# One hybrid decoder layer: index keys and queries projected first, scores inside the third chunk, top-k rounds spread over the projection chunks

## The chip, the cores and the metric

The kernel runs on one core of one Trainium2 chip. The metric is the device time of one execution in microseconds (us), median of the runs of a kernel. Five engines work side by side, each through its own instructions in order: TensorE (PE in the profile, its weight loads PEld), VectorE (DVE), ScalarE (ACT), GpSimd (POOL) and SyncE (SP), which here only issues DMAs. They wait for each other through semaphores alone.

## The reference, cut to what matters

One layer over x (1, 512, 1024): h = RMSNorm(x), one projection h @ w_in of 7,000-odd columns, three token mixers side by side, gates, two output products. Mixer A picks keys with a small indexer; its part is

```python
A_HEADS, A_HEAD_DIM, IDX_HEADS, IDX_DIM, TOPK_MAX = 4, 64, 8, 64, 256
a_q, a_ckv, a_qi, a_ki, a_wi, a_z = split_cols(a_part, A_COLS)
topk = min(TOPK_MAX, s // 4)                                  # 128 of 512
idx_logits = jnp.einsum('bqhd,bsd->bqhs', qib, k_idx) * (IDX_DIM ** -0.5)
score = jnp.einsum('bqh,bqhs->bqs', wb * (IDX_HEADS ** -0.5), jax.nn.relu(idx_logits))
score = jnp.where(key_pos[None, None, :] <= t[None, :, None], score, NEG_INF)
_, sel = lax.top_k(score, topk)
kg, vg = k[bidx, sel], v[bidx, sel]                           # then softmax over the picked keys
```

Mixer B is a gated DeltaNet (a short causal convolution over 12 x 128 features, then a chunked delta rule over 4 chunks of 128 tokens), mixer C an attention over compressed, selected and windowed keys. Everything of A's selection is used only in A's attention, near the end.

## The kernel before

The order of the work is written out by hand, engine by engine, in one function `trunk`. Nothing is scheduled by a program, so each engine does exactly what stands in its block, in that order.

**Projections.** The columns of w_in are cut into chunks of 260 to 512 columns (`CHUNKS`). A chunk has four pieces of weights. For each piece SP loads it into one of three `stage` buffers (`load`), ScalarE scales it and rounds it to float16 (`hi_split`, L688 and L693), GpSimd subtracts to get the rest (`lo_split`, L459), and TensorE multiplies with both parts (`project`, `product`, L1443 to L1445: three matmuls for each of 8 slices, four tiles t = 0 to 3 for a chunk). After tile t of a chunk ScalarE drains its bank (`drain`) and then splits pieces of the next chunk (`FOLLOW`: one, one, two, none). The order of the chunks before is C0, C1, A0, QI, A2, B0, B1, B3, B4, B2, then six gate chunks (L1656 to L1660) that serve as filler (`fill`) in the DeltaNet and attention stages. QI holds the index queries, A2 the index keys (`kiT`) and index weights.

**Banks.** PSUM has eight banks. TensorE uses them in rings of two: `S` (banks 0 and 1, drained by ScalarE), `G` (2 and 3), `V` (4 and 5, drained by VectorE) and `O` (6 and 7). Every use of a ring has a number. `v_bank(name)` makes TensorE wait until VectorE has drained the use two places before, and `filled(name)` makes VectorE wait until that use is written. So TensorE can be at most two uses of `V` ahead of VectorE.

**Uses of V in the projections.** In order: transposes of the C queries and keys (`cqT0`, `cqT1`, `kcmp`, `vcmp`, `ksT`, `kwT`), `ckvT`, `qT0`, `qT1`, four key-and-value products `ukv` (L1547, copied out by L1009 and L1010), `kT0`, `kT1` (scaled out by L1026), `kiT` (L1027), eight `flip` products that reverse the bias strips (L1562, copied out by L1029), the compressed keys and values `cmpkv` (L1577, L1065), `kcT`, and `sums`, the bank of the square sums and cumulative decays (L1619, L1633, L1634). `phi` (L1517) is a small product between tiles that uses banks 2 and 3.

**Index scores.** After B0, TensorE makes 24 products of index queries and keys (L1572: 8 heads for each of three query blocks q = 1, 2, 3 with 256, 384 and 512 keys) in ring S; ScalarE takes the ReLU into one of two buffers (L681), VectorE multiplies with the weight and adds (L1039, L1041). GpSimd masks the diagonal (L510).

**Top-k.** `topk(q)` takes 16 rounds for each q: the eight largest of a row (`max`, L1084), then their places marked (`match_replace`, L1087, which also issues a MATCH_VALUE_LOAD); each waits for the one before it. Two closing operations (L1091, L1092) make the mask `keep_add`. Before, q = 1 stands between the convolutions of B0 and B1, q = 2 and q = 3 stand in the DeltaNet: 16 and 6 half rounds ahead of its start (`TOPK_A`, `TOPK_B`), the rest one by one between the steps of a level (`between_steps`).

**Convolutions.** `conv(m)` is one L1055 and three L1057 on VectorE, then a SiLU on ScalarE (L756); conv(0) to conv(3) need B0, 4 to 7 need B1, 8 to 11 need B2. `conv(m)` waits for the SiLU of m - 2.

**Start of the DeltaNet.** After the square sums, VectorE works through a chain of small operations (L1129 to L1146), `difference(0)` (L1160), conv(8) to conv(11), `decayed_products(0)` and `level_zero(0)` (L1179), which TensorE waits for before the first level (L1588).

Of the kernel before, what the change touches and what calls it, by code (L numbers as in the profile page):

```python
# [8 lines left out]
P = 128  # L9
T, D = 512, 1024  # L10
NT, KC = T // P, D // P
EPS = 1e-6
NEG = -1e30
# [22 lines left out]
    ("w_in", C_BASE, 448), ("w_in", C_VSEL, 460),  # L36
    ("w_in", A_Q, 384), ("w_in", A_QI, 512), ("w_in", A_KI, 328),
# [10 lines left out]
(CH_C0, CH_C1, CH_A0, CH_QI, CH_A2, CH_PK, CH_PV, CH_B0, CH_B1, CH_B3, CH_B4, CH_B2,  # L48
# [7 lines left out]

FILL_Z, FILL_U, FILL_X, FILL_T = 7, 2, 7, 3

TOPK_A, TOPK_B = 16, 6
# [9 lines left out]
def shape_constants():  # L69
# [13 lines left out]
    m = np.zeros((P, 2 * LEVELS, P), np.float16)  # L83
# [39 lines left out]
def trunk(nc, x, norm_g, w_in, a_kv_norm, a_w_ukv, a_q_norm, a_k_norm, b_conv, b_a_log, b_dt_bias, b_out_norm,  # L123
# [3 lines left out]
    u8 = mybir.dt.uint8  # L127
    ALU = mybir.AluOpType
# [3 lines left out]
    with ctx:  # L132
# [58 lines left out]
        mask_halves = late[:, 3456:3456 + LEVELS * P].bitcast(f16).rearrange("p (n m) -> p n m", m=P)  # L191
# [13 lines left out]
        scores = [late[:, 0:256], late[:, 3072:3456], early[:, 4608:5120]]  # L205
        topk_work = [early[:, 5120:5632], early[:, 5632:6144]]
# [22 lines left out]
        s_names = [(c, t) for c in ("C0", "C1", "A0", "QI", "A2", "B0") for t in range(4)]  # L229
        s_names += [("idx", q, h) for q in range(1, NT) for h in range(IDX_HEADS)]  # L230
        s_names += [(c, t) for c in ("B1", "B3", "B4", "B2") for t in range(4)]
# [8 lines left out]
        v_names += ["cqT0", "cqT1", "kcmp", "vcmp", "ksT", "kwT"]  # L240
        v_names += ["ckvT", "qT0", "qT1"] + [("ukv", t) for t in range(NT)] + ["kT0", "kT1", "kiT"]
# [20 lines left out]
        O = Uses(banks[6:8], [("os", c) for c in range(1, NT)] + [("oc", n) for n in range(2)] + [("o", *g) for g in groups])  # L262
# [27 lines left out]
        T_IN = Steps(sem("transpose_input_ready"), ["C0q", "C0blk", "C0ks", "C1kw", "A0ckv", "A0q", "Ak", "Aki", "kc"])  # L290
# [60 lines left out]
        order = [(c, j) for c in range(CH_A2 + 1) for j in range(4)]  # L351
        for v, c in ((CH_PK, CH_B0), (CH_PV, CH_B1)):
            order += [(v, 0), (c, 0), (v, 1), (c, 1), (v, 2), (c, 2), (c, 3), (v, 3)]
        order += [(c, j) for c in range(CH_B3, len(CHUNKS)) for j in range(4)]
# [43 lines left out]
        def _(sp):  # L398
# [18 lines left out]
            for n in range(piece_at[CH_WO0, 0]):  # L417
                if n == piece_at[CH_C1, 3]:
# [3 lines left out]
                h = n - piece_at[CH_QI, 0]  # L422
# [5 lines left out]
                if n == piece_at[CH_A0, 2]:  # L428
                    sp.dma_start(mask_halves, masks).then_inc(masks_loaded, 16)
# [15 lines left out]
        def _(gp):  # L445
# [23 lines left out]
            for j in range(4):  # L469
                lo_split(CH_C0, j)  # L470
# [3 lines left out]
            for t in range(4):  # L474
                follow(CH_C0, t)
# [17 lines left out]
            for t in range(4):  # L493
                follow(CH_QI, t)
# [4 lines left out]
            for c in (CH_A2, CH_B0):  # L499
                for t in range(4):  # L500
                    follow(c, t)
                if c == CH_A2:

                    gp.wait_ge(masks_loaded, 16)
                    hold(gp.tensor_copy(level_masks[:, :, :], mask_halves))

            for q in range(1, NT):
                gp.wait_ge(score_ready, q)
                d = scores[q - 1][:, P * q:P * q + P]
                gp.affine_select(out=d, in_=d, compare_op=ALU.is_ge, fill=NEG, base=0, pattern=[[-1, P]],  # L510
                                 channel_multiplier=1).then_inc(diag_ready, 1)
# [11 lines left out]
            def masked_decays(c):  # L523

                gp.wait_ge(exp_ready, c + 1)
                hold(gp.tensor_tensor(decay_k, decay, over_heads(tri), ALU.mult))
# [115 lines left out]
        def _(act):  # L642
# [71 lines left out]
            def h_hi(t):  # L714
                for a in range(2):
                    if t < 2:
                        hi_split(CH_C0, 2 * t + a)
# [6 lines left out]
            for t in range(4):  # L724
                drain(("C0", t), raw_c0[:, t, :], 448, scale=1.0 / W_SCALE)
                follow(CH_C0, t)
                if t == 0:
                    h_hi(3)
# [5 lines left out]
            drain_chunk(CH_QI, "QI", lambda t: qiT[:, t, :], 384)  # L734
            drain_chunk(CH_A2, "A2", lambda t: raw_a2[:, t, :], 328)
            sqrt("Ak", ss_k, 16)
            act.wait_ge(fills, 3)
            drain_chunk(CH_B0, "B0", lambda t: qkvT[:, t, 3:T + 3])
            act.wait_ge(hid_filled, 1)
            for h in range(2):  # L740
                ins = nc.scalar.activation(hidT[:, h::2, :], banks[2 + h][:, 0:2 * N_CMP].rearrange("p (v n) -> p v n", v=2), ACT.Silu)
            ins.then_inc(hid_ready, 1)

            n = 0
            for q in range(1, NT):
# [132 lines left out]
        def _(ve):  # L878
# [141 lines left out]
            for a in range(2):  # L1020
                ins = ve.tensor_copy(ki2[:, :, a, :], raw_a2[:, :, 0:64])
# [834 lines left out]
```

## Time and profile before

| | us |
|---|---|
| median of 3 runs | 718.66 |
| lowest, highest | 716.79, 718.68 |
| the profiled execution | 722.38 |
| its span, first to last instruction | 720.5 |
| TensorE busy in it | 655.4 |
| VectorE busy in it | 451.1 |
| ScalarE, GpSimd busy in it | 310.6, 233.1 |

The profile is of one execution. Its span is 1.9 us shorter than that execution's device time, and the execution is 3.7 us above the median. Busy time is the sum over an engine's instructions; matmuls are pipelined, so the end of one is modelled and overlaps the start of the next by about 0.16 us in the timelines. What a wait is put down to is inferred from semaphores; "DVEq" is VectorE's own sequencer, which passes a semaphore on.

### The profile page before, as it was taken

How to read it: one execution, taken by the hardware profiler on the slowest of the kernel's cores; microseconds unless marked ns; L12 is line 12 of the kernel's file. 1: busy time of each engine (PE TensorE's matmuls, PEld its weight loads, DVE VectorE, ACT ScalarE, POOL GpSimd, SP SyncE). 2: the span in 40 equal slices, each digit the busy share in tenths (PEclk: the TensorE clock that was granted, in tenths of full speed). 3: DMA queues.
4: the chain of work that ended last, by engine and by line, in shares of the span. 5: the costliest groups of instructions: out<-in, count | busy, mean ns of one | idle time of the engine just before them, and what ended most of it. 6: DMA issues, size and time to landing. Idle time of an engine off the chain costs nothing.

```text
span 720.5 us, 9726 instructions
## 1 busy us (share of the span) xinstructions
PE 655.4 (91%) x3650; PEld 396.6 (55%) x3650; DVE 451.1 (63%) x897; ACT 310.6 (43%) x502; POOL 233.1 (32%) x165
## 2 busy tenths in 40 slices
PE   2799899999999984989999999999999999788898
PEld 1345556654358642767676787655555556433343
DVE  6623442314799989887878655335777775689711
ACT  3554442424556844604415122544555545253510
POOL 1353533312044644313434301434321121132530
PEclk9999899999999997999999989899999999999999
DMA  7235414532024202010200201100110120242221
GB/s 272 79 118 169 144 50 144 160 106 71 2 60 131 89 30 88 4 56 0 89 30 10 80 1 30 59 30 30 60 31 30 58 60 1 58 176 87 88 88 59
DMA packets 31191, 52.78 MB, mean 73 GB/s; under 512 B 2759, under 2 KB 13345, under 8 KB 31145
## 3 DMA queue, kind: packets, MB, share of 16 engines
q1 hardware_dynamic: 29552, 51.19, 22.6%
q10 hardware_dynamic: 1593, 0.97, 0.5%
q8 instruction: 29, 0.48, 0.3%
q14 instruction: 17, 0.14, 0.1%
HBM read 50.04 MB, written 2.12 MB: 72 GB/s over the span
## 4 chain that ended last, share of the span: by engine, by line
PE 63%; DVE 26%; issue 4%; ACT 3%; DMA 2%; POOL 1%; SPq 0%; DVEq 0%; ACTq 0%
PE bank L1588 7%; PE bank L1443 7%; PE bank L1444 7%; PE bank L1445 7%; PE bank L1656 5%; PE bank L1658 5%; PE bank L1660 5%; PE bank L1746 5%; PE bank L1763 4%; DVE early L1057 4%; DVE early L1087 3%; DVE small L1084 3%; DVE work L1179 3%; PE bank L1517 2%; PE bank L1782 2%
## 5 line engine op out<-in xcount | busy, mean ns | idle before, releaser
L459 POOL TENSOR_TENSOR w_lo<-stage,w_hi 128x1024 f16<-128x1024 f32 (+5 forms) x80 | 159.2, 1996 | 259.2 <-ACT w_hi L693 258.9
L1588 PE MATMUL bank<-work 128*128 128x128 f32 x616 | 81.3, 282 | 11.7 <-DVEq L1154 11.4
L1588 PEld LDWEIGHTS bank<-work 128*128 128x128 f32 x616 | 77.1, 195 | 23.7 <-DVEq L1154 17.9
L693 ACT ACTIVATE w_hi<-stage 128x1024 f16<-128x1024 f32 (+5 forms) x80 | 78.3, 979 | 19.9 <-issue 14.9
L688 ACT ACTIVATE stage<-stage 128x1024 f32<-128x1024 f32 (+5 forms) x80 | 77.4, 968 | 3.3 <-DMA stage<-in_w_in 3.3
L1656 PE MATMUL bank<-hT_hi,w_hi 128*128 128x512 f16 x192 | 74.6, 388 | 1.7 <-PE bank L1660 0.6
L1658 PE MATMUL bank<-hT_lo,w_hi 128*128 128x512 f16 x192 | 74.5, 388 | 0.5
L1660 PE MATMUL bank<-hT_hi,w_lo 128*128 128x512 f16 x192 | 74.3, 387 | 0.3
L1443 PE MATMUL bank<-w_hi,hT_hi 128*128 128x260 f16 (+4 forms) x192 | 62.0, 323 | 6.0 <-DVE hT_lo L923 3.0
L1444 PE MATMUL bank<-w_lo,hT_hi 128*128 128x260 f16 (+4 forms) x192 | 61.6, 321 | 0.0
L1445 PE MATMUL bank<-w_hi,hT_lo 128*128 128x260 f16 (+4 forms) x192 | 61.6, 321 | 0.0
L841 ACT ACTIVATE late<-late,small 128x128 f32<-128x128 f32 (+3 forms) x48 | 26.8, 558 | 53.7 <-DVE small L1325 53.7
L1443 PE MATMUL bank<-hT_hi,w_hi 128*128 128x512 f16 (+1 forms) x128 | 49.0, 383 | 0.8 <-ACT qkvT L681 0.4
L1444 PE MATMUL bank<-hT_lo,w_hi 128*128 128x512 f16 (+1 forms) x128 | 49.1, 383 | 0.0
L1445 PE MATMUL bank<-hT_hi,w_lo 128*128 128x512 f16 (+1 forms) x128 | 48.8, 382 | 0.0
L1179 DVE COPY_PREDICATED work<-level_masks,bank 128x512 f32<-128x512 uint8 x48 | 35.1, 732 | 21.4 <-PE bank L1588 14.6
L1361 DVE RECIPROCAL qkvT<-qkvT 128x128 f32<-128x128 f32 x48 | 45.7, 953 | 1.6
L681 ACT ACTIVATE late<-bank 128x256 f32<-128x256 f32 (+3 forms) x72 | 31.1, 449 | 17.4 <-PE bank L1572 9.7
L1057 DVE SCALAR_TENSOR_TENSOR early<-qkvT,par,early 128x512 f32<-128x512 f32 x36 | 36.7, 1019 | 1.3
L710 ACT ACTIVATE early<-bank 128x512 f32<-128x512 f32 x12 | 7.2, 597 | 67.8 <-PE bank L1660 67.8
L1443 PE MATMUL bank<-strips,w_hi 128*128 128x512 f16 x64 | 25.1, 392 | 9.7 <-DVE qkvT L1388 4.2
L1322 DVE CUSTOM_DVE_ANT_0 late<-bank,strips 128x128 f32<-128x128 f32 (+3 forms) x36 | 16.9, 469 | 25.7 <-PE bank L1746 23.6
(281 smaller groups left out, 1183.6 us busy)
## 6 DMA issues: line engine op xcount, KB each, us to landing
stage<-in_w_in SPq DMA_DIRECT2D x40, 512.0 KB, 3.5
stage<-in_c_phi_w SPq DMA_DIRECT2D x8, 512.0 KB, 3.9
stage<-in_w_branch SPq DMA_DIRECT2D x8, 512.0 KB, 3.7
stage<-in_w_out SPq DMA_DIRECT2D x8, 512.0 KB, 3.7
stage<-in_w_in SPq DMA_DIRECT2D x8, 260.0 KB, 2.8
strips<-rel_rows SPq DMA_DIRECT2D x8, 256.0 KB, 4.0
late<-in_x SPq DMA_DIRECT2D x1, 2048.0 KB, 8.9
out_x<-late SPq DMA_DIRECT2D x8, 256.0 KB, 2.2
```

The costliest lines, as they stand in the source:

```text
L459: gp.tensor_tensor(piece_view(w_lo[:, k % PAIRS, :], c), piece_view(stage[:, piece_at[c, j] % STAGES, :], c), piece_view(w_hi[:, k % PAIRS ...
L688: nc.scalar.activation(full, full, ACT.Copy, scale=W_SCALE).then_inc(scaled, 1)
L693: nc.scalar.activation(piece_view(w_hi[:, k % PAIRS, :], c), full, ACT.Copy).then_inc(hi_ready, 1)
L1057: ins = ve.scalar_tensor_tensor(acc, qkvT[:, m, w:w + T], tap[w], acc, ALU.mult, ALU.add)
L1179: return ve.copy_predicated(dst, level_masks[:, n, :].unsqueeze(1).to_broadcast([P, 4, P]), src)
L1443: mm(ps, lhs[0], rhs[0], start=start, stop=False)
L1444: mm(ps, lhs[0], rhs[1], start=False, stop=False)
L1445: return mm(ps, lhs[1], rhs[0], start=False, stop=stop)
L1588: ins = mm(ps[:, h * P:(h + 1) * P], lhs(h), rhs(h), start=True, stop=True)
L1656: mm(G.bank(g)[:, :], w[0], h[0], start=k == 0, stop=False)
L1658: mm(G.bank(g)[:, :], w[0], h[1], start=False, stop=False)
L1660: ins = mm(G.bank(g)[:, :], w[1], h[0], start=False, stop=k == KC - 1)
```

## The change

- The chunks A2 (index keys and weights) and QI (index queries) are projected first. The order is A2, QI, C0, C1, A0, B0, B1, B3, B4, B2. The orders of loads, of ScalarE's and of GpSimd's splits follow. The weights of `phi` are loaded among the pieces of B1 and B3 (before, of B0 and B1), and its products stand between the tiles of B0 and B1 (before, of A2 and B0).
- The 24 index products stand inside C0: after each of the first four slices of its tiles 0, 1 and 2, two of them, in ring O instead of S. Before C0, TensorE waits for the transposed index keys.
- The C transposes stand after tiles 2 and 3 of A0, `ckvT` after tile 2 of B0, `qT0`, `qT1` and all four `ukv` after tile 3 of B0, `kT0` and `kT1` after tile 1 of B1, the flips after its tiles 2 and 3, four each. `cmpkv` follows B3, `kcT` follows B4.
- A round of top-k is one step (max and match together), a q has 17 steps. They stand on VectorE as 17 after the scores (all of q = 1), 8 after the A0 queries are normalised, 6 between the `qT` and `ukv` copies, 6 after the `ukv` copies, 6 after the `kT` copies, and the last 8 after the flips. None is left in the DeltaNet. The buffers of scores and rounds move from `early` to `late`; `masked_decays(0)` on GpSimd waits for the last round.
- conv(0) and conv(1) stand ahead of the `kT` copies, conv(2) and conv(3) among the flip copies, conv(4) and conv(5) ahead of `cmpkv`, conv(6) and conv(7) behind its chain. The square root `kc` on ScalarE stands after tile 1 of B4.
- The level masks are loaded as uint8 straight into place, at B0; before, as float16 with a cast on GpSimd (L505).

```diff
-    ("w_in", C_BASE, 448), ("w_in", C_VSEL, 460),
-    ("w_in", A_Q, 384), ("w_in", A_QI, 512), ("w_in", A_KI, 328),
+    ("w_in", A_KI, 328), ("w_in", A_QI, 512),
+    ("w_in", C_BASE, 448), ("w_in", C_VSEL, 460), ("w_in", A_Q, 384),
...
+TOPK_C, TOPK_A0, TOPK_UKV, TOPK_AK, TOPK_KT = 17, 8, 6, 6, 6
...
-TOPK_A, TOPK_B = 16, 6
...
+            def index_relu(n):
+                q, h = idx_units[n]
+                if n >= 2:
+                    act.wait_ge(relu_used, n - 1)
+                L = P * (q + 1)
+                act.wait_ge(o_filled, O.filled(("idx", q, h)))
+                nc.scalar.activation(relu_buf[n % 2][:, 0:L], O.bank(("idx", q, h))[:, 0:L], ACT.Relu).then_inc(o_drained, 1)
+
             for t in range(4):
+                for n in range(8 * t, min(8 * t + 8, len(idx_units))):
+                    index_relu(n)
                 drain(("C0", t), raw_c0[:, t, :], 448, scale=1.0 / W_SCALE)
...
+            drain_chunk(CH_B1, "B1", lambda t: qkvT[:, 4 + t, 3:T + 3], between=lambda t: silus(t, {1: (0, 1), 2: (2,), 3: (3,)}))
...
+            def between_b4(t):
+                silus(t, {0: (4, 5), 2: (6, 7)})
+                if t == 1:
+                    sqrt("kc", ss_kc[0:N_CMP, :], 1)
...
+            def topk_all():
+
+                for q in range(1, NT):
+                    ve.wait_ge(diag_ready, q)
+                    src = scores[q - 1]
+                    for r in range(TOPK // 8):
+                        m8 = max8[:, 8 * (r % 2):8 * (r % 2) + 8]
+                        hold(ve.max(m8, src))
+                        dst = topk_work[r % 2][:, 0:P * (q + 1)]
+                        hold(ve.match_replace(dst, m8, src, TAKEN))
+                        src = dst
+                        yield
...
+            topk(TOPK_A0)
             ve.tensor_scalar(ckvT, filled("ckvT")[:, :], par[:, R_CKV:R_CKV + 1], None, ALU.mult).then_inc(v_drained, 1)
...
+            topk(TOPK_UKV)
...
+            topk(TOPK_AK)
             SQ.wait(ve, "Ak")
...
+            conv(0)
+            conv(1)
...
+            topk(TOPK_KT)
+            conv(2)
             for h in range(N_HEADS):
                 ve.tensor_copy(strips[:, h, :], filled(("flip", h))[:, :]).then_inc(v_drained, 1)
+                if h == N_HEADS // 2 - 1:
+                    conv(3)
...
+            for _ in topk_steps:
+                pass
+            conv(4)
+            conv(5)
...
+            def index_products(t, k):
+                if t == 3 or k > 3:
+                    return
+                for q, h in idx_units[8 * t + 2 * k:8 * t + 2 * k + 2]:
...
+            project(CH_C0, "C0", True, within=index_products)
```

VectorE around the copies of `ukv`. Before, the two `qT` copies, then the copies of the four products (L1009 and L1010 for each), in banks 4 and 5:

```order
L1001 TENSOR_SCALAR work<-bank5,par 128x512
L1003 TENSOR_SCALAR qT_a<-bank4,par 128x512
L1003 TENSOR_SCALAR qT_a<-bank5,par 128x512
L1009 COPY work<-bank4 128x256
L1010 COPY v_a<-bank4 128x256
L1009 COPY work<-bank5 128x256
```

In the change, the same place (L1070 is `qT`, L1077 and L1078 are the copies; the left-out rows are four more rounds like the two shown):

```order
L1070 TENSOR_SCALAR qT_a<-bank5,par 128x512
L1070 TENSOR_SCALAR qT_a<-bank4,par 128x512
L971 MAX small<-late 128x8
L973 MATCH_REPLACE late<-small,late 128x384
...
L971 MAX small<-late 128x8
L973 MATCH_REPLACE late<-small,late 128x384
L1077 COPY work<-bank5 128x256
L1078 COPY v_a<-bank5 128x256
```

Six rounds now stand between a drain of banks 4 and 5 and the next. TensorE at that place in the change (L1479 the `qT` transposes, L1566 `ukv`):

```order
L1479 MATMUL bank5<-consts,work 128x128 x4
L1479 MATMUL bank4<-consts,work 128x128 x4
L1566 MATMUL bank5<-work 128x512
L1566 MATMUL bank4<-work 128x512
L1566 MATMUL bank5<-work 128x512
L1566 MATMUL bank4<-work 128x512
L1443 MATMUL bank0<-hT_hi,w_hi 128x512
```

Its four products stand in a row, as before, but the tile of projection between the two transposes is gone, and B1's first tile stands behind them.

VectorE from the `kT` copies to the flip copies, before (L1026 `kT`, L1027 `kiT`, L1029 flips):

```order
L1026 TENSOR_SCALAR kT_a<-bank4,par 128x512
L1026 TENSOR_SCALAR kT_a<-bank5,par 128x512
L1027 COPY work<-bank4 128x512
L1029 COPY strips<-bank5 128x512
L1029 COPY strips<-bank4 128x512
```

and in the change (L957 and L959 are a convolution, L1089 `kT`, L1093 flips; the left-out rows are four more rounds):

```order
L957 TENSOR_SCALAR early<-qkvT,par 128x512
L959 SCALAR_TENSOR_TENSOR early<-qkvT,par,early 128x512 x3
L1089 TENSOR_SCALAR kT_a<-bank5,par 128x512
L1089 TENSOR_SCALAR kT_a<-bank4,par 128x512
L971 MAX small<-late 128x8
L973 MATCH_REPLACE late<-small,late 128x512
...
L971 MAX small<-late 128x8
L973 MATCH_REPLACE late<-small,late 128x512
L957 TENSOR_SCALAR early<-qkvT,par 128x512
L959 SCALAR_TENSOR_TENSOR early<-qkvT,par,early 128x512 x3
L1093 COPY strips<-bank5 128x512
```

Two convolutions came ahead of the `kT` copies, and six rounds and a convolution between them and the first flip copy.

## Rows read from the trace of the kernel before

**Rows 1.** TensorE's waits: waiting line, releaser, us in total, times, longest.
```profile
PE bank L1588 <- DVEq L1154: 11.4, 5, 7.6
```

**Rows 2.** Stretches: length, engines' busy time (instructions), granted clock, DMA share, GB/s.
```profile
98.50:172.50 74.00, 72.23 (x417) 44.52 (x415) 18.91 (x32) 27.64 (x37) 24.77 (x13) 0.98 0.43 126
...
172.50:191.00 18.50, 15.28 (x54) 7.00 (x54) 13.43 (x23) 10.01 (x24) 0.58 (x2) 1.00 0.04 14
...
284.00:288.00 4.00, 4.00 (x15) 2.44 (x15) 3.75 (x6) 1.02 (x2) 0.30 (x1) 0.55 0.38 127
```

**Rows 3.** TensorE's timeline: start, us, instruction, count, idle before and releaser.
```profile
283.57 2.08 PE L1588 MATMUL bank<-work 128*128 128x128 f32 x8 [7.59 <-DVEq L1154]
285.44 0.63 PE L1656 MATMUL bank<-hT_hi,w_hi 128*128 128x512 f16 x1
...
319.74 1.13 PE L1588 MATMUL bank<-work 128*128 128x128 f32 x8
...
321.14 0.38 PE L1656 MATMUL bank<-hT_hi,w_hi 128*128 128x512 f16 x1
```

**Rows 4.** Line L1084 and L1087 on VectorE: ns min/median/max, first to last start.
```profile
L1084 DVE MAX8 small<-early x46: 428/561/697, 209.2 to 396.6; 128x8 f32<-128x512 f32 x16, 128x8 f32<-128x256 f32 x15, 128x8 f32<-128x384 f32 x15
...
L1087 DVE MATCH_REPLACE8 early<-small,early x46: 408/543/678, 209.7 to 397.4; 128x512 f32<-128x512 f32 x16, 128x256 f32<-128x256 f32 x15, 128x384 f32<-128x384 f32 x15
```

**Rows 5.** VectorE's timeline: a round at 384 columns, and the next's start.
```profile
244.53 0.56 DVE L1084 MAX8 small<-late 128x8 f32<-128x384 f32 x1
...
245.78 0.56 DVE L1084 MAX8 small<-early 128x8 f32<-128x384 f32 x1
```

**Rows 6.** Timelines around the `ukv` products: TensorE, then VectorE.
```profile
107.94 4.11 PE L1547 MATMUL bank<-work 128*128 128x512 f32 x8
...
108.14 0.75 DVE L1003 TENSOR_SCALAR qT_a<-bank,par 128x512 f32<-128x512 f32 x1 [3.71 <-PE bank L1479]
109.07 0.42 DVE L1009 COPY work<-bank 128x256 f32<-128x256 f32 x1 [0.18 <-PE bank L1547]
...
114.84 1.22 DVE L1012 TENSOR_REDUCE small<-early 128x16 f32<-128x1024 f32 x1 [2.00 <-POOL early L498]
```

**Rows 7.** Timelines, B0's tile 1 to the flips: TensorE, then VectorE.
```profile
143.90 0.38 PE L1443 MATMUL bank<-hT_hi,w_hi 128*128 128x512 f16 x1
...
149.08 1.87 PE L1517 MATMUL bank<-early,stage 128*128 128x31 f32 x16
150.78 3.02 PE L1562 MATMUL bank<-strips,work 128*128 128x512 f32 x6
...
151.92 0.69 DVE L1029 COPY strips<-bank 128x512 f32<-128x512 f32 x1 [7.13 <-PE bank L1562]
```

**Rows 8.** Timelines at convolutions: VectorE, then a weight split on GpSimd.
```profile
228.70 4.07 DVE L1057 SCALAR_TENSOR_TENSOR early<-qkvT,par,early 128x512 f32<-128x512 f32 x3
232.69 0.48 DVE L1055 TENSOR_SCALAR early<-qkvT,par 128x512 f32<-128x512 f32 x1
233.21 2.33 DVE L1057 SCALAR_TENSOR_TENSOR early<-qkvT,par,early 128x512 f32<-128x512 f32 x3
...
229.15 2.29 POOL L459 TENSOR_TENSOR w_lo<-stage,w_hi 128x1024 f16<-128x1024 f32 x1 [4.27 <-ACT w_hi L693]
```

**Rows 9.** Timelines from `sums` to level zero: TensorE, then VectorE.
```profile
255.24 0.40 PE L1633 MATMUL bank<-small,consts 128*128 128x16 f32 x2 [1.03 <-DVEq L1125]
255.49 0.37 PE L1634 MATMUL bank<-small,ones 128*128 128x16 f32 x2
...
259.03 0.23 DVE L1129 COPY small<-bank 128x64 f32<-128x64 f32 x1
...
281.40 2.03 DVE L1179 COPY_PREDICATED work<-level_masks,work 128x512 f32<-128x512 uint8 x1
```

**Rows 10.** Page, part 6: DMA issues of weight pieces, KB each, us to landing.
```profile
stage<-in_w_in SPq DMA_DIRECT2D x40, 512.0 KB, 3.5
```

More of the change, by code:

```diff
@@ L127, in trunk @@
     u8 = mybir.dt.uint8
+    idx_units = [(q, h) for q in range(1, NT) for h in range(IDX_HEADS)]
     ALU = mybir.AluOpType
@@ L493, in _ @@
             for t in range(4):
-                follow(CH_QI, t)
+                follow(CH_B0, t)
             gp.wait_ge(v_drained, V.filled(("ukv", 3)))
@@ new lines, in _, with topk @@
+            topk_steps = topk_all()
+            def topk(n):
+                for _ in range(n):
+                    next(topk_steps)
+            ve.wait_ge(s_drained, S.filled(("A2", 3)))
+            ki2 = squares[:, 1024:1536].rearrange("p (t a d) -> p t a d", t=NT, a=2)
+            for a in range(2):
+                ins = ve.tensor_copy(ki2[:, :, a, :], raw_a2[:, :, 0:64])
+            ins.then_inc(T_IN.sem, 1)
+            hold(ve.tensor_scalar(raw_a2[:, :, 64:72], raw_a2[:, :, 64:72], IDX_HEADS ** -0.5, 64 ** -0.5, ALU.mult, ALU.mult))
@@ new lines, in _ @@
+            ve.tensor_copy(kiT, filled("kiT")[:, :]).then_inc(v_drained, 1)
+            ve.wait_ge(v_drained, V.filled("kiT"))
+            n = 0
+            for q in range(1, NT):
+                L = P * (q + 1)
+                for h in range(IDX_HEADS):
+                    ve.wait_ge(o_drained, O.filled(("idx", q, h)))
+                    r, wi = relu_buf[n % 2][:, 0:L], raw_a2[:, q, 64 + h:65 + h]
+                    if h == 0:
+                        ins = ve.tensor_scalar(scores[q - 1], r, wi, None, ALU.mult)
+                    else:
+                        ins = ve.scalar_tensor_tensor(scores[q - 1], r, wi, scores[q - 1], ALU.mult, ALU.add)
+                    n += 1
+                    ins.then_inc(relu_used, 1)
+                    ve.wait_ge(relu_used, n)
+                ve.nop().then_inc(score_ready, 1)
@@ L1117, in _ @@
             ve.nop().then_inc(GATE_IN.sem, 1)
-            for _ in range(TOPK_A):
-                next(topk_last)
+            ve.tensor_scalar(kcT[:, 0:N_CMP], filled("kcT")[:, 0:N_CMP], par[:, R_CK:R_CK + 1], None, ALU.mult).then_inc(v_drained, 1)
             GATE_OUT.wait(ve, "sp")
@@ L1125, in _ @@
             ve.nop().then_inc(gsum_ready, 1)
-            for _ in range(TOPK_B):
-                next(topk_last)
             ps = filled("sums")
@@ L1643, in _ @@
             project(CH_B4, "B4", True, between=between_b4)
+            T_IN.wait(pe, "kc")
+            transposes("kcT", [raw_c0[0:N_CMP, 0, 0:128]], N_CMP)
             project(CH_B2, "B2", False, between=between_b2, within=within_b2)
```

257 lines of the change are left out of this document (100 added, 157 removed).

## Prediction

> **What bounds the kernel now.** I read the shares of busy time first: TensorE is busy 655.4 of a span of 720.5 us, VectorE 451.1. So an edit counts only by what it does to TensorE's idle time. Then its waits: only five, 11.4 us in all, lie in the DeltaNet on VectorE's vector work, and one of them is 7.6 [rows 1]. Then the stretches that the change touches. Over 98.5 to 172.5 TensorE works 72.23 of 74.0 us and VectorE only 18.91; in the index scores TensorE works 15.28 of 18.50 [rows 2]. The tempting reading is that VectorE has 55 us to give away ahead of the scores. The other question is when VectorE must answer: TensorE may be only two uses of ring V ahead, and VectorE takes its instructions in order, so rounds put before a drain are paid for by whatever TensorE cannot cover with other work.
>
> **What a wait costs beyond itself.** After the 7.59 us wait TensorE's next two groups took 2.08 and 0.63 us, where elsewhere they took 1.13 and 0.38 [rows 3], and over the next 4 us the granted clock was 0.55 [rows 2], its lower level (1.2 GHz) for most of it. That is 4 x 0.45 = 1.8 us and 0.2 for the half us ahead of it: 2.0 us behind a long wait. I charge it to each wait of over 5 us.
>
> **What a round costs.** A max and a match have medians of 561 and 543 ns [rows 4]; a round of 384 columns has a pitch of 1.25 us [rows 5], so waits and the value load add 0.13. At 256 columns (0.43 + 0.41, row minima) it is 0.98, at 512 (0.70 + 0.68, maxima) 1.53. The last of a q also has two closing operations, about 0.8 (an estimate, two passes like those of a round at 384 columns, less their wait).
>
> **Wait A, `ukv`.** The two `qT` copies (0.75) are followed at once by the first `ukv` copy (0.42) in the trace; the four products take 4.11, 1.03 each [rows 6]. In the change six rounds (6 x 1.25 = 7.5) stand between. TensorE can write two products and must then wait for the copies of the first. From the second `qT` copy: VectorE 7.5 + 0.8 = 8.3, TensorE 1.0. +7.3, with the clock **+9.3**. Nothing covers it: the projection tile between the two transposes is gone, too.
>
> **Wait B, the flips.** From the last `ukv` product on, VectorE has its copies 0.8; two rounds 2.5, closing 0.8, three rounds 4.6; the key norms, with two passes of 1.22 [rows 6] and a root, about 4; conv(0) and conv(1); two `kT` copies 1.5; six rounds 9.2; conv(2); one flip copy 0.7 [rows 7]. A convolution is 0.48 + 2.28 = 2.76, from the 2.33 of three steps; beside a GpSimd split (2.29) the three took 4.07, so 1.74 more [rows 8]. With one such split that is 34.2 us. TensorE ahead of its third flip has three tiles of 5.2 (143.90 to 149.08 is one), three `phi` of 1.7, `kT` 0.9 and two flips of 0.95 [rows 7]: 23.5. +10.7, with the clock **+12.7**. Before, VectorE stood idle 7.13 us ahead of that copy, so this is a lead turned into a lag.
>
> **Wait C, `sums`.** Its bank is free only when `cmpkv` is copied. After the flips VectorE has seven more rounds 10.7, closing 0.9, conv(4) and conv(5) 5.5 with one split 1.75, and the copies: about 20. TensorE has B3, four tiles of 260 columns (5.2 x 260 / 512 = 2.64 each), `cmpkv` and flip rests 0.9, and B4's first tile 2.64: 14.1. +5.9, with the clock **+7.9**.
>
> **D, the root `kc`.** ScalarE takes it only after B4's tile 1, so VectorE, which has just caught up, stands still before conv(6) and conv(7); ScalarE's SiLU of those stands before its drain of B4's tile 3. From TensorE's release in C: root at about 7.5 (tile 1, drain, split: estimated), rest of the chain 1, two convolutions with one split 7.3, SiLUs and drain 2.0: 17.8. TensorE: sums 1.0, three tiles 7.9, `kcT` 0.3, B2's tile 0 5.2: 14.4. +3.4, and 0.9 for a last piece of B2 whose ScalarE half is late: **+4.3**, from 0 to 6.
>
> **Index scores.** The 3.2 us of waits [rows 2] go and another 0.3 of overlap with C0's slices; new are ScalarE's weight splits ahead of a ReLU at tiles 1 and 2, and VectorE's accumulations beside GpSimd's splits. By rows 8 the nearest such meeting cost 1.74; bounds 0.5 and 3, I take 1.7. **-1.8**. What the trace shows here is the 4.07 against 2.33 [rows 8]: steps with two inputs in SBUF slow down beside GpSimd, and the one-input L1055 at 232.69 ran 0.48. The Trainium skill, page "SBUF — State Buffer", section "Who interferes with whom", states just that: two SBUF inputs contend with a GpSimd instruction that reads SBUF, one input does not. It speaks against moving the scores beside C1's and C0's splits; without it this term would be about -3.0, with it -1.8.
>
> **Start.** The first chunk has 120 columns less, one tile of it 1.2 us shorter (5.2 x 120 / 512) before the second can wait for weights: -1.2. QI's last piece (load 3.5 [rows 10], GpSimd split 2.29) queues behind GpSimd's other splits: +1.5. TensorE waits for the `kiT` copy before C0: 0.7 and its semaphores, +1.0. **+1.3**, from -1 to +3, since no row shows this order.
>
> **What goes.** The small waits of 98.5 to 172.5 are 74.0 - 72.2, **-1.8** [rows 2], as their drains lie elsewhere. The VectorE chain that ends in level zero (283.43) began on `sums` at 259.03 though TensorE had it ready at 255.86, and TensorE had waited 1.03 for the bank [rows 9]: half rounds stood in between and are gone, **-4.2**. The rest of that chain stays, so TensorE still waits some us for level zero. The other four DeltaNet waits are 11.4 - 7.6 = 3.8 [rows 1]; no round is left in those stages: **-3.5**. The other rounds removed there are worth nothing, as TensorE works through them. Masks as uint8, the loads' order and the steps of a round: nothing, all behind TensorE's work (a mask load that came late would hold level zero; it has over 100 us).
>
> **Sum.** 9.3 + 12.7 + 7.9 + 4.3 = 34.2; -1.8 + 1.3 - 1.8 - 4.2 - 3.5 = -10.0; +24.2. Against the profiled 722.4 that is 746.6. That execution is 3.7 above the median of 718.7; on the median's basis **742.9**.
>
> **The rivals.** *Shorter waits*: the three waits come, but the clock does not drop behind them and D finds cover: 24.2 - 6.0 - 4.3 = 13.9, 732.6. For: 7.6 us is the only wait whose clock I can read. Against: nothing differs in kind.
>
> *Longer*: up to six more GpSimd splits fall on convolutions and accumulations, 6 x 1.74 = 10.4: 753. For: GpSimd splits nearly without a pause in the projections. Against: half of VectorE's new work there is rounds, and rows 4 show none slowed by more than a fourth.
>
> *Faster, the other side*: VectorE drains each bank before TensorE comes. It rests on one balance, wait B's 34.2 against 23.5; it turns if rounds and convolutions there take under two thirds of my price, or TensorE's share is half as large again. Then A and C, smaller balances of the same kind, would vanish first, and only -10.0 is left: 708.7. For: VectorE's 18.91 of 74.0 [rows 2]. Against: the listed instructions, each with its row.
>
> *Cancelling*: A alone comes at full size (TensorE has nothing else there) and meets the gains: 9.3 - 10.0, 718.
>
> **How the numbers follow.** Forecast 742.9 with its own range 735 to 750, chance 0.60; shorter 728 to 735, 0.17; longer to 753, 0.11; faster 0.07; cancelling 0.05. The range takes the first three, 728 to 753. A measurement of this kernel tells about 0.3% (2.2 us) from no change: faster 0.07, same 0.03 (most of cancelling), slower 0.90.
>
> **What would show it.** In the changed kernel's trace: the third `ukv` product idle about 7 us before it, the third flip about 11, the first square sum after B4's tile 0 about 6, B2's tile 1 about 3; a low clock for some 4 us behind each of the first three; the DeltaNet's waits down from 11.4 to about 8; under 2 us of idle between the index products. I would be wrong in kind if TensorE shows no wait on VectorE at these places, and in size if convolutions measure far from 2.76 or rounds from 1.25.

## The result and the profile after

The changed kernel takes 741.25 us (median of 4 runs, 739.46 to 741.38) against 718.67 before: a ratio of 1.0294, 95% interval 1.0251 to 1.0336, slower by 22.6 us. The forecast was 742.9 with a range of 728 to 753. The profiled execution of the change is 739.46 us, its span 737.6, against 722.38 and 720.5 before: the two traces differ by 17.1, the medians by 22.6. Some executions of a kernel are slower by a per cent or two as a whole, at a lower granted clock (728.27 among those before); medians here are of all executions, ratios and intervals of the undisturbed ones alone.

The page has the same work and more idle time: TensorE 654.2 us busy (655.4 before), in a span 17.1 longer.

```profile
span 737.6 us, 9700 instructions
...
PE 654.2 (89%) x3650; PEld 398.5 (54%) x3650; DVE 449.8 (61%) x897; ACT 310.2 (42%) x502; POOL 236.9 (32%) x164
```

TensorE's waits of the change (waiting line, releaser, total, times, longest) answer to [rows 1]; the longest, 10.8 us for a DMA near the start, is left out, since the kernel before has it too (10.6). L1566 is `ukv`, L1580 the flips, L1628 the first square sums, L1443 with `raw_b` is B2's tile 1, L1597 the DeltaNet.

```profile
PE bank L1580 <- DVE strips L1093: 10.2, 1, 10.2
PE bank L1597 <- DVEq L1159: 8.8, 3, 7.6
PE bank L1566 <- DVE v_a L1078: 6.8, 1, 6.8
PE bank L1628 <- DVE cmp_v L1105: 6.0, 1, 6.0
...
PE bank L1443 <- ACT raw_b L678: 3.6, 1, 3.6
```

The four new waits are there with sizes near the computed ones (7.3, 10.7, 5.9 and 3.4). TensorE's timeline of the change shows each, and what the next group took:

```profile
164.19 1.96 PE L1566 MATMUL bank<-work 128*128 128x512 f32 x4 [0.50 <-DVE qT_a L1070]
172.92 3.43 PE L1566 MATMUL bank<-work 128*128 128x512 f32 x4 [6.78 <-DVE v_a L1078]
...
197.75 1.96 PE L1580 MATMUL bank<-strips,work 128*128 128x512 f32 x4
209.91 3.71 PE L1580 MATMUL bank<-strips,work 128*128 128x512 f32 x4 [10.20 <-DVE strips L1093]
...
244.98 6.99 PE L1628 MATMUL bank<-ones,early 128*128 128x1 f32 x32 [6.02 <-DVE cmp_v L1105]
...
273.69 0.39 PE L1443 MATMUL bank<-hT_hi,w_hi 128*128 128x512 f16 x1 [3.63 <-ACT raw_b L678]
...
308.80 2.08 PE L1597 MATMUL bank<-work 128*128 128x128 f32 x8 [7.59 <-DVEq L1159]
```

The same two products take 1.96 us ahead of a wait and 3.43 or 3.71 behind it. The last row answers to the first of [rows 3]: the first level begins at 308.80 instead of 283.57, 25.2 us later, with the same 7.59 us of waiting ahead of it.

### The profile page after: what moved, and what is told of

It reads as the page before. It is cut to its first block, busy times and chain, and to the rows that moved or that the text cites. A ratio compares the mean times of both kernels' runs of the same rounds, so it can differ in the third digit from the quotient of the medians.

```text
span 737.6 us, 9700 instructions
## 1 busy us (share of the span) xinstructions
PE 654.2 (89%) x3650; PEld 398.5 (54%) x3650; DVE 449.8 (61%) x897; ACT 310.2 (42%) x502; POOL 236.9 (32%) x164
## 4 chain that ended last, share of the span: by engine, by line
PE 70%; DVE 21%; issue 3%; ACT 2%; DMA 1%; POOL 1%; SPq 0%; DVEq 0%; ACTq 0%
PE bank L1597 11%; PE bank L1443 8%; PE bank L1445 7%; PE bank L1444 7%; PE bank L1667 6%; PE bank L1669 6%; PE bank L1671 5%; PE bank L1757 5%; PE bank L1774 4%; DVE early L959 4%; DVE late L973 2%; DVE small L971 2%; PE bank L1793 2%; PE bank L1479 2%; PE bank L1628 1%
## 5 line engine op out<-in xcount | busy, mean ns | idle before, releaser
L457 POOL TENSOR_TENSOR w_lo<-stage,w_hi 128x1024 f16<-128x1024 f32 (+5 forms) x80 | 162.3, 2036 | 297.6 <-ACT w_hi L690 297.6
L690 ACT ACTIVATE w_hi<-stage 128x1024 f16<-128x1024 f32 (+5 forms) x80 | 78.3, 979 | 32.7 <-issue 28.7
L1597 PE MATMUL bank<-work 128*128 128x128 f32 x616 | 79.4, 278 | 9.1 <-DVEq L1159 8.8
L1597 PEld LDWEIGHTS bank<-work 128*128 128x128 f32 x616 | 77.1, 193 | 17.7 <-DVEq L1159 10.7
L1443 PE MATMUL bank<-w_hi,hT_hi 128*128 128x260 f16 (+4 forms) x192 | 63.3, 330 | 3.6 <-DVE hT_lo L928 2.2
L1443 PE MATMUL bank<-hT_hi,w_hi 128*128 128x512 f16 (+1 forms) x128 | 47.3, 370 | 6.5 <-ACT raw_b L678 3.6
L1445 PE MATMUL bank<-hT_hi,w_lo 128*128 128x512 f16 (+1 forms) x128 | 47.3, 370 | 0.0
L1444 PE MATMUL bank<-hT_lo,w_hi 128*128 128x512 f16 (+1 forms) x128 | 47.3, 370 | 0.0
L959 DVE SCALAR_TENSOR_TENSOR early<-qkvT,par,early 128x512 f32<-128x512 f32 x36 | 39.9, 1108 | 1.3
L1443 PE MATMUL bank<-strips,w_hi 128*128 128x512 f16 x64 | 24.9, 389 | 9.3 <-DVE qkvT L1388 4.2
L1322 DVE CUSTOM_DVE_ANT_0 late<-bank,strips 128x128 f32<-128x128 f32 (+3 forms) x36 | 16.9, 469 | 26.7 <-PE bank L1757 24.6
L1443 PEld LDWEIGHTS bank<-w_hi,hT_hi 128*128 128x128 f16 x192 | 19.7, 103 | 22.5 <-issue 8.8
```

The costliest lines, as they stand in the source:

```text
L457: gp.tensor_tensor(piece_view(w_lo[:, k % PAIRS, :], c), piece_view(stage[:, piece_at[c, j] % STAGES, :], c), piece_view(w_hi[:, k % PAIRS ...
L690: nc.scalar.activation(piece_view(w_hi[:, k % PAIRS, :], c), full, ACT.Copy).then_inc(hi_ready, 1)
L959: ins = ve.scalar_tensor_tensor(acc, qkvT[:, m, w:w + T], tap[w], acc, ALU.mult, ALU.add)
L1443: mm(ps, lhs[0], rhs[0], start=start, stop=False)
L1444: mm(ps, lhs[0], rhs[1], start=False, stop=False)
L1445: return mm(ps, lhs[1], rhs[0], start=False, stop=stop)
```

## Why TensorE waits there

VectorE's timeline of the change, from the `qT` copies to the copies of `ukv`: the start of the first and the whole of the last of the six rounds, which fill 164.62 to 172.07, and then the first of the two copies for which TensorE waits.

```profile
163.29 1.41 DVE L1070 TENSOR_SCALAR qT_a<-bank,par 128x512 f32<-128x512 f32 x2 [6.92 <-PE bank L1479]
164.62 0.55 DVE L971 MAX8 small<-late 128x8 f32<-128x384 f32 x1
...
170.86 0.56 DVE L971 MAX8 small<-late 128x8 f32<-128x384 f32 x1
171.46 0.09 DVE L973 MATCH_VALUE_LOAD late<-small,late 128x8 f32 x1
171.53 0.54 DVE L973 MATCH_REPLACE8 late<-small,late 128x384 f32<-128x384 f32 x1
172.11 0.42 DVE L1077 COPY work<-bank 128x256 f32<-128x256 f32 x1
```

VectorE stood idle for 6.92 us just ahead of the `qT` copies, and then started six rounds when TensorE needed it. The pitch (from one round's start to the next's) is 1.25, as in [rows 5]. The second place is in front of B2, on VectorE and then on ScalarE:

```profile
245.44 0.14 DVE L897 TENSOR_SCALAR small<-small 31x1 f32<-31x1 f32 x1
261.19 0.15 DVE L904 RECIPROCAL small<-small 31x1 f32<-31x1 f32 x1 [15.60 <-ACT small L674]
```

```profile
257.22 0.39 ACT L678 ACTIVATE raw_b<-bank 128x260 f32<-128x260 f32 x1 [11.89 <-PE bank L1445]
...
260.96 0.20 ACT L674 ACTIVATE small<-small 31x1 f32<-31x1 f32 x1
```

VectorE asked for the root `kc` at 245.44 and had it at 261.19. ScalarE was idle for 11.89 us of that, since tile 1's drain stands ahead of the root in its order, and TensorE, released from its wait at 244.98, ended tile 1 only at 257.2: the square sums and the tile, both at a low clock, took 12.2 us.

## Experiments

The runs that change one thing start from the changed kernel (741.2). Each was run beside the kernel before, whose medians were 718.5, 721.5 and 718.3 in the three sets, so a difference of under 2 or 3 us between kernels of different sets tells nothing.

### The six rounds put behind the `ukv` copies

```diff
-TOPK_C, TOPK_A0, TOPK_UKV, TOPK_AK, TOPK_KT = 17, 8, 6, 6, 6
+TOPK_C, TOPK_A0, TOPK_UKV, TOPK_AK, TOPK_KT = 17, 8, 0, 12, 6
```

> The changed kernel with one move on VectorE: the six rounds between the qT and the ukv copies stand behind the ukv copies, with the six that are there already. Theory (VectorE is late as a whole from ukv to the flips, so rounds moved within that stretch only move the wait): the wait before the third ukv product falls from 6.8 us to under 0.5, and its low clock (1.5) goes, but the wait before the third flip grows from 10.2 by the six rounds, 7.5, to about 17.7; net -0.6 to -1.5, about 740 us against the changed kernel's 741.2. Rival (each drain behind rounds costs by itself, the flips have cover for more): 741.2 - 8.3 = 733.

Measured 741.62 us, ratio 1.0353 (1.0286 to 1.042). TensorE's timeline (the last row ends where its view ended; the fourth product is not in it):

```profile
168.04 4.00 PE L1566 MATMUL bank<-work 128*128 128x512 f32 x8 [0.50 <-DVE qT_a L1070]
192.09 1.97 PE L1479 MATMUL bank<-consts,work 128*128 128x128 f32 x8 [6.28 <-DVE work L1085]
213.09 2.92 PE L1580 MATMUL bank<-strips,work 128*128 128x512 f32 x3 [8.52 <-DVE strips L1093]
```

The wait at `ukv` is gone and stands elsewhere: 6.3 ahead of the `kT` transposes, whose norms VectorE computes late, and 8.5 at the flips, 14.8 in all against 17.0. The rival's 733 lies outside the interval. The theory held in sum; that a part would fall on `kT` was not foreseen.

### The six rounds put ahead of the `qT` copies

```diff
+            topk(TOPK_UKV)
             for m in range(2):
                 ve.tensor_scalar(qT_a[:, m, :], filled(f"qT{m}")[:, :], ...
...
-            topk(TOPK_UKV)
```

> The changed kernel with the same six rounds moved the other way, ahead of the qT copies, where VectorE stands idle 6.9 us (156.4 to 163.3). Theory (what costs is the place behind which VectorE cannot catch up): the 6.8 us wait and 1.5 us of low clock go, the rounds (7.5) overrun the idle stretch by 0.6; the other waits stay as they are: 741.2 - 8.3 + 0.6 = 733.5 us. Rival (VectorE has too much work in sum, the wait turns up at qT or at the flips): 740 to 741.

Measured 736.03 us, ratio 1.0274 (1.0198 to 1.035). The wait at `ukv` is gone, the wait ahead of the first product is 1.0 instead of the change's 0.5, and the waits at flips and sums are unchanged (10.2 and 6.0). The gain of 5.2 lies nearer the theory, but runs of 731.2 to 741.5 do not exclude the rival by time; the waits do.

### Half of them

Three rounds ahead of the `qT` copies, three left.

> The changed kernel with three of the six rounds ahead of the ukv copies put ahead of the qT copies: half of wait A. Theory: the wait before the third ukv product is what the rounds ahead of it take, less one product: 6.8 - 3.75 = 3.0 us, and the other three rounds lie in VectorE's idle 6.9 us, free. If a wait of 3 us costs no low clock behind it, the kernel gains 3.75 + 1.5 + 0.5 (the wait that was 0.5 ahead of it stays): 736; if it costs the same low clock, 3.75: 737.5. Rival (the wait has another cause than these rounds): 6 us or more stay, 741.

Measured 734.65 us, ratio 1.0221 (1.016 to 1.0281). The row of the wait in TensorE's timeline, and under it windows of 4 us (length, busy time of PE, PEld, DVE, ACT and POOL, granted clock, DMA share, GB/s):

```profile
168.68 3.49 PE L1567 MATMUL bank<-work 128*128 128x512 f32 x4 [3.02 <-DVE v_a L1079]
```

```profile
163.00:167.00 4.00, 2.08 (x6) 0.67 (x4) 3.86 (x9) 0.00 (x0) 0.00 (x0) 1.00 0.70 198
167.00:171.00 4.00, 2.32 (x3) 1.18 (x4) 2.42 (x8) 0.00 (x0) 0.00 (x0) 0.67 0.00 0
```

The wait is 3.0, as computed: round for round. The two products behind it still took 3.49, so this 3 us wait cost 1.5 of low clock too. The time alone would say the contrary (736 without that cost, 737.5 with it), but it also lies below that of the kernel with all six rounds moved, so differences of this size are not told apart by it; the row decides.

### The root `kc` earlier

```diff
-                if t == 1:
+                if t == 0:
                     sqrt("kc", ss_kc[0:N_CMP, :], 1)
```

> The changed kernel with one move on ScalarE: the square root kc stands after tile 0 of B4 instead of tile 1. Theory: VectorE no longer stands still for 15.6 us ahead of conv(6) and conv(7), so their SiLUs no longer hold ScalarE's drain of B4's tile 3; TensorE's waits at B2's tile 1 (3.6) and for the last weight piece of B2 (1.1) go, with the low clock behind them (about 2.5): -4.7 to -7.2, 734 to 736.5 us. Rival (the drain is late through ScalarE's own queue of splits, not through kc): within 1 us of 741.2.

Measured 733.49 us, ratio 1.0255 (1.0179 to 1.0331), 7.8 below the change and a little more than the 4.7 to 7.2 expected. Both waits in B2 are gone from the trace; wait C stands at 6.0 as before. The rival falls.

### The rounds spread over VectorE's idle stretches, and with the early root

```diff
-TOPK_C, TOPK_A0, TOPK_UKV, TOPK_AK, TOPK_KT = 17, 8, 6, 6, 6
+TOPK_C, TOPK_A0, TOPK_UKV, TOPK_AK, TOPK_KT = 17, 8, 5, 3, 1
...
-            y, w = inv_root("C0", ss_c, 20, 1.0 / 64)
+            ve.tensor_scalar(ss_c, ss_c, 1.0 / 64, EPS, ALU.mult, ALU.add).then_inc(ROOT_IN.sem, 1)
+            topk(4)
+            y, w = newton_root("C0", ss_c, 20)
...
+            topk(4)
             for m in range(2):
                 ve.tensor_scalar(qT_c[:, m, :], filled(f"cqT{m}")[:, :], ...
+            topk(3)
             for v, name in enumerate(("kcmp", "vcmp")):
...
+            topk(TOPK_UKV)
             for m in range(2):
                 ve.tensor_scalar(qT_a[:, m, :], filled(f"qT{m}")[:, :], ...
...
-            topk(TOPK_UKV)
```

> The changed kernel with its rounds put where VectorE stands idle in its trace: 17 after the scores as now, 4 while the root of C0 is taken, 4 ahead of the cqT copies, 3 ahead of the kcmp blocks, 8 after the A0 queries as now, 5 ahead of the qT copies, then 3 behind the ukv copies, 1 behind the kT copies, the last 6 behind the flips; kc as it is. Theory: wait A (6.8 + 1.5) goes; ahead of the flips VectorE has 23.2 us against TensorE's 23.5, so wait B (10.2 + 1.8) goes or is under 1; wait C falls from 6.0 to about 3; B2's waits stay. 741.2 - 8.3 - 12 - 3 to -6 = 715 to 718 us. Rival (VectorE's work in sum is too much for the projections wherever it stands): waits of the same sum at other places, over 730.

Measured 716.98 us, ratio 0.9999 (0.9968 to 1.003). Waits A and B are gone and C is 2.5. Between 160 and 240 us the only wait over 0.5 us other than C's is this one (behind it stand B2's 1.1 and 3.6, since the root is where it was):

```profile
164.32 4.00 PE L1570 MATMUL bank<-work 128*128 128x512 f32 x8 [1.07 <-DVE qT_a L1075]
```

The same 51 steps and the same chunk order, with only VectorE's order changed, take back the whole loss.

With the edit of the early root added:

> The spread rounds (17, 4, 4, 3, 8, 5 ahead of ukv, 3, 1, 6 behind) and the root kc behind tile 0 of B4, together. Theory (the causes add, being at different places): the spread kernel's median is 717.0, and the early root took 7.8 us off the changed kernel, of which 4.7 are waits and the rest low clock: 717.0 - 5 to -8 = 709 to 712 us, faster than before (718.5). Rival (the early root pays only where wait C stands ahead of it): 716 to 717.

Measured 709.06 us, ratio 0.9854 (0.9801 to 0.9907): the two causes add (716.98 less 709.06 is 7.9, the early root alone took off 7.8), and this version beats both kernels, the one before by about 1.5%.

### Without rounds

The 48 max and 48 match of a kernel are left out; every other instruction stays. No keys are picked then, so the result differs from the layer's; the runs serve for timing alone.

> The kernel before with its top-k rounds left out, 48 max and 48 match_replace (the closing operations stay, on unpicked scores). It tells what the rounds cost where they stood. Theory of the prediction: the DeltaNet's waits fall by 3.5 and the chain from sums to level zero starts 4.2 us earlier: 718.5 - 7.7 = 711 us. Rival (the trace of the change showed the DeltaNet stage 9.7 us shorter, all of it from the rounds): 718.5 - 9.7 - 4.2 = 705. Rival (VectorE's rounds there were free): 716 to 718.5.

Measured 712.77 us in the median (707.15 to 718.93), ratio 0.9841 (0.9748 to 0.9933).

> The changed kernel with its top-k rounds left out, 48 max and 48 match_replace (the closing operations stay, on unpicked scores). It tells what the reorder costs without them. Theory: waits A, B and C are made by the rounds (without them VectorE has about 17 us against TensorE's 23.5 ahead of the flips, 8 against 14 ahead of sums), and go with their low clock, 8.3 + 12 + 6 to 11; the late root kc stays: 741.2 - 26 to -31 = 710 to 715 us. Rival (the convolutions ahead of kT and cmpkv, or the order of chunks, make a part of the waits): 720 to 730.

Measured 710.47 us, ratio 0.9892 (0.9824 to 0.9961). In its trace the waits at `ukv`, flips and sums are all gone and the 3.6 at B2 stays. So the rounds make A, B and C, their places as the spread shows, and the convolutions and the chunk order alone do not. How much the rounds cost in the kernel before, 8 or 14 us, this interval does not settle, and the two kernels without rounds can't be told apart.

### The square sums a tile later

```diff
                 if t == 0:
                     v_bank("sums")
+                if t == 1:
                     square_sums(range(4))
```

> The changed kernel with one move on TensorE: it still waits for the sums bank after tile 0 of B4 (6.0 us), but the 32 small products of the first square sums, which ran at a granted clock of 0.50 from 244.9 to over 252, stand after tile 1, so that the wait is followed by the dense products of tile 1. Theory (small products leave the clock low; dense ones get it back in about 4 us, as behind the other waits): the low clock behind C costs 2 instead of about 6.5 us, -3 to -4.5, 737 to 738 us. Rival (the clock stays low for a time of its own after such a wait, whatever follows): within 1 us of 741.2.

Measured 734.2 us, ratio 1.0237 (1.0155 to 1.0319), 7.0 below the change, more than theory or rival said. The windows of the change behind wait C first, then two of this kernel:

```profile
244.90:248.90 4.00, 3.92 (x19) 3.92 (x19) 0.58 (x4) 0.43 (x1) 0.00 (x0) 0.50 0.47 135
248.90:252.90 4.00, 4.00 (x21) 3.67 (x21) 0.00 (x0) 0.00 (x0) 0.00 (x0) 0.50 0.00 0
252.90:256.90 4.00, 4.00 (x20) 2.83 (x19) 0.00 (x0) 0.00 (x0) 0.00 (x0) 0.50 0.00 0
```

```profile
248.00:252.00 4.00, 4.00 (x36) 3.73 (x34) 0.00 (x0) 2.25 (x3) 0.00 (x0) 0.93 0.00 0
252.00:256.00 4.00, 4.00 (x21) 3.41 (x21) 2.10 (x9) 1.63 (x3) 2.12 (x1) 0.50 0.16 19
```

With the dense tile next, the clock is back by 248.5. It falls again in the square sums, and its two low stretches cost TensorE 5.0 us together, as the one stretch in the kernel with the early root did. What the 7.0 came from is seen beside that kernel, in which TensorE's order is that of the change. From the release behind wait C to the small product of the `kcT` transpose, first there, then here:

```profile
245.21 6.99 PE L1628 MATMUL bank<-ones,early 128*128 128x1 f32 x32 [6.03 <-DVE cmp_v L1105]
...
262.08 0.21 PE L1479 MATMUL bank<-consts,early 31*128 31x31 f32 x1 [0.30 <-PE bank L1445]
```

```profile
245.33 0.40 PE L1443 MATMUL bank<-w_hi,hT_hi 128*128 128x260 f16 x1 [6.03 <-DVE cmp_v L1105]
...
262.10 0.21 PE L1479 MATMUL bank<-consts,early 31*128 31x31 f32 x1 [0.30 <-PE bank L1445]
```

That is 16.9 us with the sums first and 16.8 with the dense tile first (18.2 in the change, 244.98 to 263.18), and the first level begins at 300.86 and 300.87. So the dense tile first gained nothing that the early root did not: here too the tile's drain and the root `kc` come before the sums, and the waits of 1.1 and 3.6 us in B2 are gone. The theory that the low clock behind C is dear because the small products stand first is not borne out: moved, they cost what they cost in the kernel with the early root.

### The index products in a row

```diff
-            project(CH_C0, "C0", True, within=index_products)
+            project(CH_C0, "C0", True)
+            for t in range(3):
+                for k in range(4):
+                    index_products(t, k)
...
-                for n in range(8 * t, min(8 * t + 8, len(idx_units))):
-                    index_relu(n)
                 drain(("C0", t), raw_c0[:, t, :], 448, scale=1.0 / W_SCALE)
                 follow(CH_C0, t)
+            for n in range(len(idx_units)):
+                index_relu(n)
```

> The changed kernel with the 24 index products in a row after C0, in ring O, instead of between C0's matmuls (ScalarE's ReLUs behind its four drains of C0 accordingly). Theory (the interleave is worth the waits of TensorE on ScalarE's ReLUs, which were 3.2 of 18.5 us in the kernel before, and 16.0 for C0's share against 18.3 in a row in the trace of the change): +2 to +3 us, 743 to 744. Rival (the chip lowers the clock among light products in a row: the kernel before without rounds showed 0.50 and 0.59 there in one profile): +6 to +10. Rival (the interleave is worth nothing): 741.

Measured 750.99 us, ratio 1.0435 (1.0376 to 1.0494), 9.7 above the change. The row's window in this kernel, then the window of C0 with the products inside, in the change:

```profile
76.30:102.20 25.90, 24.45 (x49) 9.81 (x49) 17.31 (x23) 11.35 (x24) 6.43 (x5) 0.61 0.26 77
```

```profile
58.70:93.60 34.90, 32.81 (x144) 13.57 (x144) 21.24 (x39) 19.73 (x36) 7.19 (x7) 1.00 0.26 81
```

In a row they take 25.9 us at a clock of 0.61; between C0's matmuls 34.9 less C0's own 18.3 (its 96 matmuls from 57.87 to 76.20 in the kernel with the row), 16.6, at full clock. The first rival held: 9.7 lies in its +6 to +10. The kernel before had them in a row at 1.00 and 18.5 us [rows 2], so the low clock does not follow from the row alone; but in the profile of that kernel without rounds the row ran at 0.50 over 182 to 198. Why it comes in one and not in another stays open.

### Two attempts at more

Both start from the kernel with the spread rounds and the early root, 709.06.

> The spread rounds with the early root kc, and besides conv(10) behind level_zero(0) instead of ahead of it, conv(11) behind level one's first three steps. Aimed at the 7.6 us for which TensorE waits at the first level in every kernel here. Theory (VectorE's chain sets the end of that wait): conv(10)'s 4.56 us (0.49 and 4.07, beside GpSimd) go from it, the wait falls to 3.0, and conv(11) costs at most 1 in the first level: 709.1 - 3.5 to -5 = 704 to 706 us. Rival (convolutions late cost the same in the first levels): 709.

```diff
             decayed_products(0)
+            level_zero(0)
             conv(10)
-            level_zero(0)
-            conv(11)
+            late_convs = [0, 1]
...
+                    if c == 0 and late_convs and late_convs.pop(0):
+                        conv(11)
```

Measured 708.98 us, ratio 0.9849 (0.9803 to 0.9894), the same as without this edit and as the rival said. TensorE's timeline at the first level:

```profile
272.87 1.16 PE L1603 MATMUL bank<-work 128*128 128x128 f32 x8 [1.76 <-DVEq L1163]
...
280.88 3.62 PE L1603 MATMUL bank<-work 128*128 128x128 f32 x16 [5.31 <-DVEq L1163]
```

The 7.6 us wait fell to 1.8, and 5.3 us turned up one product later, behind conv(10): the wait moved by one step.

> As the kernel with level_zero first, and besides the last three of the 51 steps (two rounds, one closing pair) stand behind the chain of kc instead of ahead of conv(4): aimed at the 2.5 us that are left of wait C. Theory: VectorE copies cmpkv 4 us earlier, the 2.5 us wait ahead of the square sums and the low clock among them go, conv(6) and conv(7) keep cover: 3 to 5 below the kernel with level_zero first, 700 to 702 us. Rival (late conv(6) and conv(7) give it back at B2's tile 1): 704 to 706.

```diff
-            for _ in topk_steps:
-                pass
+            topk(3)
             conv(4)
             conv(5)
...
+            for _ in topk_steps:
+                pass
             conv(6)
```

Measured 714.75 us, ratio 0.998 (0.9931 to 1.0028). Wait C is gone, and B2's tile 1 waits 3.6 again, in TensorE's timeline and then VectorE's at conv(6):

```profile
245.25 0.39 PE L1450 MATMUL bank<-hT_hi,w_hi 128*128 128x512 f16 x1 [3.63 <-ACT raw_b L678]
```

```profile
232.83 7.82 DVE L959 SCALAR_TENSOR_TENSOR early<-qkvT,par,early 128x512 f32<-128x512 f32 x3
```

The rival held and was priced too low, 714.75 for 704 to 706: conv(6) not only started later, its three steps, 2.33 alone, took 7.82 beside GpSimd's splits.

## Point by point

**What bounds it.** Right. The balance of VectorE's list against TensorE's cover decided, not VectorE's share of busy time. At wait B the list ran from 176.4 to 209.8, 33.4 us against the 34.2 of the sum, TensorE's side 23.4 against 23.5.

**Waits A and B.** A measured 6.8 and 1.5 of low clock, 8.3 for 9.3. B 10.2 and 1.75, 12.0 for 12.7.

**Wait C.** The wait is 6.0 for 5.9, but its clock was under-sized: the 32 square sums took 6.99 where they took 3.96 in the kernel before, and tile 1 5.4 instead of the 2.64 of a tile at full clock, so 5.8 for 2.0. The step that failed is the flat 2.0 us behind a wait. It was read off a place where dense products follow.

**D, the root `kc`.** The waits are 3.6 for 3.4 and 1.1 for 0.9, but the first of these is luck. From TensorE's release in C to the drain's end at 273.6 the chain took 28.7 us where the sum has 17.8, and TensorE's own work took about 24 where it has 14.4: the working counts 1.0 for the square sums, which took 6.99, leaves them out of the root's 7.5 us (the root ended 16.2 behind the release), and has one split beside the two convolutions, whose steps took 5.82 and 3.18. Both sides were 10 short, and the difference came out. The early root took 7.8 off where 4.3 was forecast (up to 6): the low clock behind these waits was left out of the term.

**Index scores.** 16.6 for the 18.5 of the row at full clock [rows 2] is -1.9 for the -1.8 of the sum, with 2.1 us of idle time for the "under 2". What the sum left out is that a row can run at a low clock; against such a row the interleave is worth 9 us. The row read for the one-input step shows nothing beside GpSimd: its split in [rows 8] ended at 231.44, the step began at 232.69. Beside a split the same step, 0.48 alone, took 1.40 in the change, VectorE and then GpSimd:

```profile
188.76 1.40 DVE L957 TENSOR_SCALAR early<-qkvT,par 128x512 f32<-128x512 f32 x1
```

```profile
188.21 1.67 POOL L457 TENSOR_TENSOR w_lo<-stage,w_hi 128x520 f16<-128x520 f32 x1 [9.09 <-ACT w_hi L690]
```

So one input did not spare it, against what the prediction says there.

**What goes.** Under-sized. The chain from `sums` is shorter by 3.2 and the wait of 1.03 is gone, the 4.2 of the sum. But the kernel before had low clock too, and I counted only idle time. Its windows behind the `kcmp` waits (1.02 and 0.66) and from a `phi` wait of 0.90 on:

```profile
85.98:92.98 7.00, 6.34 (x23) 3.54 (x24) 4.32 (x8) 0.00 (x0) 2.75 (x1) 0.52 0.27 91
```

```profile
131.40:135.40 4.00, 3.99 (x23) 2.66 (x24) 2.75 (x3) 1.15 (x3) 3.21 (x2) 0.83 0.45 134
```

Up to the first level the account is this, with the low clock added up over windows of half a microsecond, TensorE's busy time times what the granted clock lacks to 1.00. The sum has 28.2 of new waits, 6.0 of low clock and -6.5 for all the rest (index scores, start, what goes), 27.7. The traces have 27.7 of new waits and 11.3 of low clock in the change, less 8.2 of low clock in the kernel before, less 5.2 of other idle time: 25.6, against the 25.2 by which the first level is later. So the low clock was wrong by 5.3 on one side and by 8.2 on the other. That the sum is near is luck in this part.

**DeltaNet and the basis.** Forecast -3.5. In the traces the stage from the first level to A's attention is 171.3 us before and 161.6 after, -9.7: idle time fell by 4.1, and 3.4 are one low-clock stretch of the profiled execution before, with TensorE busy throughout. Here is its window:

```profile
421.00:437.00 16.00, 16.00 (x102) 12.77 (x101) 7.73 (x16) 8.03 (x11) 0.00 (x0) 0.79 0.00 1
```

The stretch does not come from the rounds: a stretch of the same size stands in the profile with the six rounds ahead of the `qT` copies, which has none left in this stage, and the stage takes 165.9 there. In the profiles of six kernels without it (the change among them) the stage takes 161.5 to 161.7. So by these traces the stretch is worth about 4.3 and the rounds 5.5, for 3.5 forecast. The stretch is about what the execution before lies above the median (3.7), so the sum made on the median's basis came out within 1.7 us while against the profiled time it would have been 7.1 too high. The choice of the basis was lucky.

**The rivals.** The faster case needed VectorE's list under TensorE's cover at the flips; it was 10 us over. "Shorter waits" failed on both conditions: the clock fell behind all waits, and D found no cover. "Cancelling" needed A to come alone. "Longer" rested on GpSimd splitting nearly without a pause; the prediction's own row has it busy for 24.77 of 74.0 us [rows 2].

## What to carry to other kernels

An idle share does not say where work fits: before work goes into an in-order engine's list, add up that list between two points where another engine waits for it, and set it against the other's own work there. Put filler ahead of an instruction that is itself waiting for input, not between an input that has arrived and the drain that others need: the same 51 steps made 741 us in one order and 717 in the other. A root or drain that one engine asks of another belongs at the other's first idle point, not behind its next tile; here that was worth 7.8 us. A stretch of low clock in one profile can come and go with the execution, so a difference between two profiles is a price only when others show it too.

## What was not expected of the hardware

Low clock follows some waits of 0.9 to 3 us too (0.52, 0.83 and 0.67 in the windows above), but not each: behind the 1.07 us wait of the spread kernel the eight products took 4.00, against 4.11 in the kernel before. It also comes without a wait. In the kernel before, the 32 square sums had none ahead of them and took 3.96 us at full clock, and then the dense tile behind them ran at 0.50 from 230 to 232.

It is not a fixed price either. Dense products had the clock back in about 3 us (245.3 to 248.5), while behind wait C the square sums and the tile after them ran at 0.50 for 12 us. The 24 index products in a row ran at 0.61 in one kernel and at 1.00 in another.

Three convolution steps, 2.33 us alone and 4.07 beside one GpSimd split [rows 8], took 5.82 in the change beside two splits (at 263.26), and 7.82 beside three in a row.
